# Late modulation vectors of a two-layer diffusion trunk: partial tiles transposed on TensorE, their four groups added by one VectorE instruction

## The chip, the cores and the metric

The kernel runs on one core of a Trainium2 chip. The metric is the device time of one execution in microseconds; the times shown are those of three executions and their median. TensorE (PE), VectorE (DVE), ScalarE (ACT), GpSimd (POOL) and SyncE (SP) each work through a list of instructions of their own and wait for each other by semaphores.

## What is computed

The reference is one step of a trunk of two layers over 384 tokens (128 of a prompt, 256 of a sample) with 1024 channels. Each layer has a token-mixing part with four branches (mLSTM, neighbourhood attention, differential attention, Mamba-2 scan) and an expert part of 16 experts. Both are modulated by six vectors per layer, which come from a conditioning vector, one for the prompt tokens and one for the sample tokens:

```python
def modulation(cvec, w_ada, b_ada):
    m = (jax.nn.silu(cvec) @ w_ada + b_ada)[:, None, :]
    return jnp.split(m, 6, axis=-1)

def trunk_layer(x, cvec, p, lam_init, ctx):
    shift1, scale1, gate1, shift2, scale2, gate2 = modulation(cvec, p['w_ada'], p['b_ada'])
    h = rms_norm(x, p['norm1_w']) * (1 + scale1) + shift1
    ...
    x = x + gate1 * (mixed @ p['w_out'])
    h2 = rms_norm(x, p['norm2_w']) * (1 + scale2) + shift2
    x = x + gate2 * expert_choice_ffn(h2, p['w_router'], p['w_gate'], p['w_up'], p['w_down'])
```

The product with w_ada (1024 by 6144) is what the change is about: columns 2048 to 6143, which give gate1, shift2, scale2 and gate2. All arithmetic is fp32 or split fp32 (a high and a low part).

## The kernel before

The kernel is written by hand for each engine; the order of the work is the order of the lines, and semaphores join the engines.

A layer runs so: modulated norm, input projection (seven tiles of w_in), neighbourhood attention (10 units), differential attention (12 units), two scans (mLSTM, SSD) with their states, the branch norms on VectorE, the transposes of the branches (L1211), the branch and output projections, the router, and 16 experts whose weights stream in by DMA.

Between the units of attention and scans TensorE takes jobs, in the order of JOB_SITES. A letter names the kind: g is one of 32 gate tiles of 128 columns (24 matmuls of the split weights, L781), p ("part") is one of eight w_ada tiles of 512 columns, s ("sum") finishes the tile of the same number. The order is s0 with the first attention unit, s1 and s2 with two later ones, s3 in the first scan, s4 at its state, s5 in the second scan, s6 at the second state, s7 in the tail, where only jobs are left on TensorE while VectorE does the branch norms.

A part (ada_partial, L787) multiplies 32 columns, of which two hold the conditioning vectors and 30 are zero, by the tile. The eight chunks of 128 rows are spread over four groups of 32 columns of the array, two chunks each, so that row 32 g + r of the bank holds group g's share for vector r. ScalarE copies the bank to SBUF (MPL). A sum (ada_sum, L793) then takes each 128 columns of that copy as weights against adasel, a constant of 128 by 2 with ones in the rows 32 g + r: this adds the four groups and turns the result, and leaves 2 columns per 128 channels, 8 in all. ScalarE copies these 8 columns to mod (take_job, L1447). The first four w_ada tiles of a layer go by ada_early and ada_select, with the same ada_sum; of the 24 sums of the program 16 are jobs.

After each gate job ScalarE (L1595) takes the result, stores it, and writes the high part of the next weight quarter (high_parts, L1447); GpSimd then subtracts it from the weights to leave the low part (L722), which TensorE needs four quarters later. ScalarE's job copies stand in its queue between the exponentials of attention and scans.

On VectorE the branch norms end at L2271 (br_ready), for which TensorE's transposes of L1211 wait. Next VectorE waits for the copy of sum 7, adds the bias to mod (L2275), forms the scale (L2277) and halves two vectors (L2278, L2279); then it forms the low parts of the transposed branches (L2286), each after ScalarE's copy of the high part, for which the branch matmuls (L781 on the operand named work_fp32r) wait. mod is next used by L2311, after the output projection. L2239 to L2271 are the last steps of the branch norms; L2260 adds the state's share of the scan to its output. rowp holds the layer's row parameters; its columns lambda and m0 (128 each) are read before the attention units begin, and the next layer's are loaded over them after the router.

Of the kernel before, what the change touches and what calls it, by code (L numbers as in the profile page):

```python
# [22 lines left out]
ALU = mybir.AluOpType  # L23
ACT = mybir.ActivationFunctionType
AX = mybir.AxisListType
# [19 lines left out]
ROW, _at = {}, 0  # L45
# [98 lines left out]
EARLY = 4  # L144
# [125 lines left out]
def trunk_program(nc, dr, outs):  # L270

    (y_prompt, y_sample, new_na_k, new_na_v, new_diff_k, new_diff_v, new_C, new_n, new_m, new_ssm) = outs
    with ExitStack() as ctx:
# [6 lines left out]
        dve_step = ctx.enter_context(nc.semaphore("dve_step"))  # L280
# [7 lines left out]
        PS = ctx.enter_context(nc.psum_tensor("banks", [128, 8, 512], F32))  # L288
# [20 lines left out]
        rowp = sb("rowp", [128, NROW])  # L309
        colp = sb("colp", [128, NCOL])  # L310
        c32 = sb("c32", [128, KC, 32])
        mod = sb("mod", [128, 48, 2])
# [9 lines left out]
        def RP(name):  # L322
            o, w = ROW[name]
            return rowp[:, o:o + w]

        def CP(name):
            o, w = COL[name]
            return colp[:, o:o + w]
# [92 lines left out]
        def MPL(i):  # L421

            return KRAW if i < 3 else NAQK[:, 1:3, 256:512]
# [84 lines left out]
        ident = K("ident")  # L508
# [3 lines left out]
        def over(ap, axis, n):  # L512

            v = ap.unsqueeze(axis)
            shape = list(v.shape)
            shape[axis] = n
            return v.broadcast_to(shape)

        def job_bank(j):

            return 3 if j == 0 else j % 2
# [248 lines left out]
        def _(pe):  # L770
# [20 lines left out]
            def ada_sum(bank, partial):  # L791
                for j in range(4):
                    mm = pe.matmul(PS[:, bank, 2 * j:2 * j + 2], partial[:, j // 2, 128 * (j % 2):128 * (j % 2) + 128], K("adasel"), start=True, stop=True)  # L793
                return mm

            def ada_early(layer, i, keys):


                for j in range(i, i + 2):
                    w = tile(keys[j - i])  # L800
                    if i:
                        pe.wait_ge(sem["ada_taken"], EARLY * layer + j - 1)
                    ada_partial(ada_bank(layer, j), w).then_inc(sem["ada_part"], 1)
# [20 lines left out]
            for g in range(6):  # L824
                t, h = g // 2, g % 2
                for c in range(4):
                    mm = pe.transpose(PS[:, g, c * 128:(c + 1) * 128], XIN[:, t, (4 * h + c) * 128:(4 * h + c + 1) * 128], ident)
# [9 lines left out]
            for l in range(L):  # L837
# [6 lines left out]
                for k in range(KC):  # L844
                    pe.wait_ge(sem["hl_odd" if k % 2 else "hl_ready"], 4 * l + k // 2 + 1)
                    mm = three_passes(PS[0:24, 7, 0:T], (WSMH[:, k, :], wsm[:, k, :]), h_in(k), k == 0, k == KC - 1)
# [52 lines left out]
                for t in range(TT):  # L899
                    mm = pe.transpose(PS[:, 7, 24 * t:24 * t + 24], GRAW[0:24, t * 128:(t + 1) * 128], ident[0:24, 0:24])  # L900
# [9 lines left out]
                for i in range(3):  # L910
                    mm = turn3(4 + i, lambda t: ROWS[:, i, t * 128:(t + 1) * 128])
# [7 lines left out]
                for c in range(4):  # L919
                    mm = pe.transpose(PS[:, 6, c * 128:(c + 1) * 128], KRAW[:, c // 2, (c % 2) * 128:(c % 2) * 128 + 128], ident)  # L920
# [4 lines left out]
                def job():  # L925

                    j = jobs[0]
                    jobs[0] += 1
                    kind, i = JOBS[j]
                    if j >= 2:  # L930
                        pe.wait_ge(sem["job_evac"], NJ * l + j - 1)
                    else:
                        pe.wait_ge(sem["proj_evac"], N_PROJ * l + (19, N_PROJ)[j])
                    if kind == "sum":
                        pe.wait_ge(sem["job_evac"], NJ * l + JOBS.index(("part", i)) + 1)
                        mm = ada_sum(job_bank(j), MPL(i))
                    elif kind == "part":
                        mm = ada_partial(job_bank(j), tile(("mix", l, 7 + [t_[:2] for t_ in JOB_TILES].index(("ada", i)))))
                    else:
                        hi, lo_ = next_quarter()[0]  # L940
                        for k in range(KC):
                            mm = three_passes(PS[:, job_bank(j), 0:T], (hi[:, k, :], lo_[:, k, :]), h_in(k), k == 0, k == KC - 1)
                    mm.then_inc(sem["job_out"], 1)
# [14 lines left out]
                for t, b in ((0, 7), (1, 4), (2, 5)):  # L958
                    for c in range(4):
                        mm = pe.transpose(PS[:, b, c * 128:(c + 1) * 128], NAQK[:, t, c * 128:(c + 1) * 128], ident)  # L960
# [177 lines left out]
                for i, (t, d, b, bq) in enumerate(((0, 0, 2, None), (0, 1, 3, None), (1, 0, 4, 5), (1, 1, 6, 7), (2, 0, 2, 3), (2, 1, 4, 5))):  # L1138
                    if i >= 4:
                        pe.wait_ge(sem["num_evac"], 9 * l + i - 2)  # L1140
                    for h in range(4):
                        mm = over_keys(PS[:, b, 65 * h:65 * h + 65], h, [(d, ks, off) for ks, off in SEEN[d][t]], lambda _, ks: V1[:, ks, h, :])
                    if bq is not None:
                        for ch in range(2):
                            mm = pe.matmul(PS[:, bq, 130 * ch:130 * ch + 130], QKT[:, ch, t * 128:(t + 1) * 128], C0[:, ch, d, :], start=True, stop=True)
# [3 lines left out]
                for c in range(2):  # L1149
                    mm = pe.transpose(PS[:, 6, c * 128:(c + 1) * 128], QKT[:, 2 + c, 0:128], ident)  # L1150
# [5 lines left out]
                for d in range(2):  # L1156
                    for h in range(4):
                        mm = pe.matmul(PS[0:64, 7 if d == 0 else 2, 65 * h:65 * h + 65], KW[:, d, h, :], V1[:, 0, h, :], start=True, stop=True)
# [28 lines left out]
                for g, b in ((0, 4), (1, 7)):  # L1187
                    for t in (1, 2):
                        o = 256 * (t - 1)
                        mm = pe.matmul(PS[:, b, o:o + 256], XS[64 * g:64 * g + 64, 3, t * 128:(t + 1) * 128], H0[64 * g:64 * g + 64, :], start=True, stop=True)  # L1190
# [254 lines left out]
        def _(act):  # L1445
            def copy(dst, src, scale=1.0):
                return act.activation(dst, src, ACT.Copy, scale=scale)  # L1447
# [48 lines left out]
            for l in range(L):  # L1496
# [29 lines left out]
                j = [0]  # L1526
# [55 lines left out]
                def take_job(split=True):  # L1582

                    j = jobs[0]
                    jobs[0] += 1
                    kind, i = JOBS[j]
                    act.wait_ge(sem["job_out"], NJ * l + j + 1)
                    if kind == "part":
                        ins = copy(MPL(i), PS[:, job_bank(j), :].rearrange("p (a b) -> p a b", a=2))
                    elif kind == "sum":  # L1590
                        ins = copy(mod[:, 4 * (EARLY + i):4 * (EARLY + i) + 4, :], PS[:, job_bank(j), 0:8].rearrange("p (a b) -> p a b", a=4))
                    else:
                        if 8 <= i:
                            act.wait_ge(spilled[i % 8], 16 * (SPILLED // 8 * l + i // 8))
                        ins = act.activation(GATES[:, i % 8, :], PS[:, job_bank(j), 0:T], ACT.Tanh, scale=0.5)  # L1595
                    ins.then_inc(sem["job_evac"], 1)
                    if j and JOBS[j - 1][0] == "gate" and JOBS[j - 1][1] < SPILLED:
                        g = JOBS[j - 1][1]
                        act.wait_ge(sem["job_evac"], NJ * l + j)
                        act.dma_start(spill[l, g % 8, :, g // 8, :], GATES[:, g % 8, :]).then_inc(spilled[g % 8], 16)  # L1600
                    if split:
                        high_parts(AHEAD[j])
# [208 lines left out]
        def _(dve):  # L1811
            steps = [0]

            def step():

                steps[0] += 1
                return steps[0]
# [28 lines left out]
            for l in range(L):  # L1846
# [425 lines left out]


                dve.wait_ge(sem["job_evac"], NJ * l + JOBS.index(("sum", 7)) + 1)
                TTo(mod[:, 16:48, :], mod[:, 16:48, :], over(CP("b_ada")[:, 16:48], 2, 2), ALU.add).then_inc(dve_step, 1)  # L2275
                dve.wait_ge(dve_step, step())
                STT(amp[:, 1, :, :], mod[:, 32:40, :], 1.0, over(CP("norm2"), 2, 2), ALU.add, ALU.mult)  # L2277
# [174 lines left out]
```

## Time and profile before

| | us |
|---|---|
| median of 3 executions | 1950.98 (1949.69 to 1955.09) |
| span of the profiled execution, first to last instruction | 1947.9 |
| TensorE busy | 1760.1 (90%) |
| VectorE busy | 639.0 (33%) |
| ScalarE busy | 548.0 (28%) |
| GpSimd busy | 514.4 (26%) |
| mean granted TensorE clock | 0.994 |

The profiled execution's own time outside the profiler isn't given; its span stands 3.1 us below the median. In the rows below times count from the span's start. A timeline row has start, duration, engine, line, operation, output and inputs, shapes, and the number of instructions that it merges; a bracket at its end is the idle time of the engine before it and what ended it. A TensorE matmul of fp32 operands is recorded as two passes, each with a weight load (PEld), a transpose as one.

### The profile page before, as it was taken

What the parts mean: (1) busy time and instruction counts of PE and PEld (TensorE: products, weight loads), DVE (VectorE), ACT (ScalarE), POOL (GpSimd) and SP (SyncE); (2) the same over time, 40 slices, a digit from 0 to 9 for tenths busy, and PEclk for the clock granted to TensorE, in tenths of its full rate; (3) what the DMA queues carried; (4) which work ended last, traced back from release to release, by engine and by line L of the source; (5) the groups of instructions that cost most, each with busy time, mean ns of one, the idle gap of its engine ahead of it and who ended that gap; (6) DMA issues with size and microseconds to landing.
All of it is one profiled execution on the core that took longest, in us unless ns stands there. A gap on an engine that the chain in (4) does not pass through costs nothing.

```text
span 1947.9 us, 22784 instructions
## 1 busy us (share of the span) xinstructions
PE 1760.1 (90%) x9204; PEld 1122.5 (58%) x9204; DVE 639.0 (33%) x1385; ACT 548.0 (28%) x1054; POOL 514.4 (26%) x654
## 2 busy tenths in 40 slices
PE   6899999999998788888889999999999988888887
PEld 3788897899442222222258889879975322222223
DVE  1187345873400000001143853558632000000011
ACT  3444444242321110110144444432442111011011
POOL 0787344275100000000037754424830000000000
PEclk9999999999999999999999999999999999999999
DMA  9525533574999999999973354345655999999996
GB/s 351 133 100 184 205 119 131 182 244 177 386 393 429 426 427 427 428 426 427 421 208 130 104 199 168 117 162 175 241 215 239 425 427 426 428 427 427 427 425 274
DMA packets 123545, 567.78 MB, mean 291 GB/s; under 512 B 21809, under 2 KB 31281, under 8 KB 98353
## 3 DMA queue, kind: packets, MB, share of 16 engines
q1 hardware_dynamic: 112656, 543.91, 70.6%
q10 hardware_dynamic: 9920, 20.84, 3.0%
q8 instruction: 73, 1.20, 0.3%
q0 software_dynamic: 864, 1.58, 0.2%
q14 instruction: 32, 0.25, 0.0%
HBM read 550.57 MB, written 15.73 MB: 291 GB/s over the span
## 4 chain that ended last, share of the span: by engine, by line
PE 53%; DMA 35%; DVE 7%; ACT 2%; SPq 1%; issue 1%; POOL 0%; ACTq 0%; DVEq 0%
PE banks L781 29%; PE banks L1342 11%; DMA work<-in_w_gate 8%; DMA ring<-in_w_down 6%; DMA ring<-in_w_up 6%; DMA work<-in_w_up 6%; DMA ring<-in_w_gate 4%; DMA work<-in_w_down 3%; PE banks L787 1%; PE banks L1091 1%; PE banks L1311 1%; DMA ring<-in_w_ada 1%; PE banks L793 1%; ACT work L1447 1%; PE banks L1107 1%
## 5 line engine op out<-in xcount | busy, mean ns | idle before, releaser
L722 POOL TENSOR_TENSOR ring_fp32r<-ring,ring_fp32r 128x256 fp32r<-128x256 f32 x592 | 462.8, 816 | 822.9 <-ACT ring_fp32r L1447 822.2
L1342 PE MATMUL banks<-ring,work 128*64 128x512 f32 x1776 | 402.7, 597 | 77.6 <-DMA ring<-in_w_gate 33.6
L781 PE MATMUL banks<-xT_fp32r,ring_fp32r 128*128 128x384 f32 x1280 | 347.6, 345 | 1.8 <-POOL ring_fp32r L722 1.8
L1447 ACT ACTIVATE work<-banks 32x512 f32<-32x512 f32 (+6 forms) x400 | 202.7, 528 | 449.3 <-PE banks L1342 251.8
L1342 PEld LDWEIGHTS banks<-ring,work 128*64 128x64 f32 x1776 | 122.4, 136 | 336.3 <-issue 198.7
L1342 PE MATMUL banks<-work 128*64 128x512 f32 x972 | 224.1, 597 | 39.2 <-DMA work<-in_w_gate 14.9
L781 PEld LDWEIGHTS banks<-xT_fp32r,ring_fp32r 128*128 128x128 f32 x1280 | 235.9, 191 | 12.8 <-issue 5.3
L781 PE MATMUL banks<-hT_fp32r,ring_fp32r 128*128 128x384 f32 x640 | 216.4, 338 | 0.0
L2364 DVE SCALAR_TENSOR_TENSOR xT<-banks,mod,xT 128x128 f32<-128x128 f32 (+1 forms) x128 | 46.7, 413 | 444.8 <-PE banks L1378 444.5
L1447 ACT ACTIVATE ring_fp32r<-ring 128x1024 fp32r<-128x1024 f32 (+1 forms) x164 | 154.4, 970 | 76.5 <-PE banks L781 66.9
L1342 PEld LDWEIGHTS banks<-work 128*64 128x64 f32 x972 | 67.1, 137 | 178.1 <-issue 111.3
L1762 ACT ACTIVATE work<-banks 128x512 f32<-128x512 f32 x32 | 19.1, 597 | 480.6 <-PE banks L1342 480.6
L781 PE MATMUL banks<-work_fp32r,ring_fp32r 128*128 128x384 f32 x768 | 139.2, 341 | 0.0
L781 PE MATMUL banks<-ring_fp32r,xT_fp32r 128*128 128x512 f32 (+1 forms) x480 | 136.2, 369 | 1.2 <-DVE small L1892 1.2
L781 PEld LDWEIGHTS banks<-work_fp32r,ring_fp32r 128*128 128x128 f32 x768 | 134.6, 189 | 2.7
L781 PEld LDWEIGHTS banks<-hT_fp32r,ring_fp32r 128*128 128x128 f32 x640 | 122.2, 191 | 1.1
L2386 DVE TENSOR_TENSOR work<-work,banks 128x512 f32<-128x512 f32 x32 | 22.0, 688 | 291.5 <-PE banks L1342 291.5
L781 PEld LDWEIGHTS banks<-ring_fp32r,xT_fp32r 128*128 128x128 f32 x480 | 86.7, 189 | 16.0 <-DVE small L1892 1.4
L1342 PE MATMUL banks<-hT,work 128*64 128x512 f32 x324 | 75.2, 599 | 20.5 <-DMA work<-in_w_gate 8.4
L781 PE MATMUL banks<-ring_fp32r,hT_fp32r 128*128 128x512 f32 (+1 forms) x240 | 88.4, 368 | 0.0
L1595 ACT ACTIVATE work<-banks 128x384 f32<-128x384 f32 x64 | 31.4, 490 | 162.1 <-PE banks L781 162.1
L1342 PEld LDWEIGHTS banks<-hT,work 128*64 128x64 f32 x324 | 21.7, 136 | 68.4 <-issue 33.3
(296 smaller groups left out, 1706.7 us busy)
## 6 DMA issues: line engine op xcount, KB each, us to landing
ring<-in_w_up SPq DMA_DIRECT2D x38, 2048.0 KB, 30.6
ring<-in_w_gate SPq DMA_DIRECT2D x37, 2048.0 KB, 30.5
ring<-in_w_down SPq DMA_DIRECT2D x36, 2048.0 KB, 30.0
ring<-in_w_in SPq DMA_DIRECT2D x28, 2048.0 KB, 8.2
ring<-in_w_ada SPq DMA_DIRECT2D x24, 2048.0 KB, 8.5
work<-in_w_down SPq DMA_DIRECT2D x20, 2048.0 KB, 30.5
work<-in_w_gate SPq DMA_DIRECT2D x18, 2048.0 KB, 30.5
work<-in_w_up SPq DMA_DIRECT2D x16, 2048.0 KB, 30.6
```

What stands on the lines that cost most here:

```text
L722: ins = pool.tensor_tensor(rounded(w_), w_, rounded(hi_), ALU.subtract)
L781: mm = pe.matmul(dst, a_, b_, start=(first and i == 0), stop=(last and i == 2))
L787: mm = pe.matmul(PS[32 * g:32 * g + 32, bank, :], c32[:, k, :], w[:, k, :], start=(k < 4), stop=(k >= 4), tile_position=(0, 32 * g))
L793: mm = pe.matmul(PS[:, bank, 2 * j:2 * j + 2], partial[:, j // 2, 128 * (j % 2):128 * (j % 2) + 128], K("adasel"), start=True, stop=True)
L1091: pe.matmul(PS[:, 4 + c % 4, 0:T], ident[:, r:r + 1].broadcast_to([128, 128]), ROWS[:, 0, :], start=True, stop=True)\
L1107: mm = pe.matmul(dst, PM[:, 2 * h + d, off:off + 128], v(d, ks), start=(i == 0), stop=(i == len(pairs) - 1))
L1311: mm = pe.matmul(dst, rounded(strided(part[:, t, 512 * (q // 8):512 * (q // 8) + 512], q // 2 % 4)), rounded(SEL[:, t, a:b, :].rearrange(" ...
L1342: mm = pe.matmul(dst[64 * hf:64 * hf + 64, :], x(k), w[kk][:, 512 * hf:512 * hf + 512], start=(k == 0), stop=(k == KC - 1), tile_position= ...
L1447: return act.activation(dst, src, ACT.Copy, scale=scale)
L1595: ins = act.activation(GATES[:, i % 8, :], PS[:, job_bank(j), 0:T], ACT.Tanh, scale=0.5)
L2364: ins = STT(xT[:, dc, a:b], PS[:, bank, a:b], mod[:, 40 + dc, g:g + 1], xT[:, dc, a:b], ALU.mult, ALU.add)
L2386: TTo(HH[:, e % 2, :], SA, PS[:, 2 * (e % 2) + 1, :], ALU.mult).then_inc(sem["hh_ready"], 1)
```

## The change

The 16 sums that are jobs become transposes. TensorE turns the four chunks of 128 columns whole (ada_turn), into the full bank. ScalarE copies columns 32 g and 32 g + 1 of each chunk, 32 columns in all, to MODP, which is the place of lambda and m0 in rowp (256 columns for eight tiles). When the eight are there, VectorE adds the four groups of all tiles into mod in one reduction, ahead of the bias. The early sums stay as they are.

```diff
--- before.py
+++ after.py
@@ -322,6 +322,8 @@
         def RP(name):
             o, w = ROW[name]
             return rowp[:, o:o + w]
+
+        MODP = rowp[:, ROW["lambda"][0]:ROW["lambda"][0] + 256]
 
         def CP(name):
             o, w = COL[name]
@@ -793,6 +795,11 @@
                     mm = pe.matmul(PS[:, bank, 2 * j:2 * j + 2], partial[:, j // 2, 128 * (j % 2):128 * (j % 2) + 128], K("adasel"), start=True, stop=True)
                 return mm
 
+            def ada_turn(bank, partial):
+                for j in range(4):
+                    mm = pe.transpose(PS[:, bank, 128 * j:128 * j + 128], partial[:, j // 2, 128 * (j % 2):128 * (j % 2) + 128], ident)
+                return mm
+
             def ada_early(layer, i, keys):
 
 
@@ -933,7 +940,7 @@
                         pe.wait_ge(sem["proj_evac"], N_PROJ * l + (19, N_PROJ)[j])
                     if kind == "sum":
                         pe.wait_ge(sem["job_evac"], NJ * l + JOBS.index(("part", i)) + 1)
-                        mm = ada_sum(job_bank(j), MPL(i))
+                        mm = ada_turn(job_bank(j), MPL(i))
                     elif kind == "part":
                         mm = ada_partial(job_bank(j), tile(("mix", l, 7 + [t_[:2] for t_ in JOB_TILES].index(("ada", i)))))
                     else:
@@ -1588,7 +1595,8 @@
                     if kind == "part":
                         ins = copy(MPL(i), PS[:, job_bank(j), :].rearrange("p (a b) -> p a b", a=2))
                     elif kind == "sum":
-                        ins = copy(mod[:, 4 * (EARLY + i):4 * (EARLY + i) + 4, :], PS[:, job_bank(j), 0:8].rearrange("p (a b) -> p a b", a=4))
+                        turned = PS[:, job_bank(j), :].rearrange("p (a b) -> p a b", a=16)[:, :, 0:2]
+                        ins = copy(MODP[:, 32 * i:32 * i + 32].rearrange("p (a b) -> p a b", a=16), turned)
                     else:
                         if 8 <= i:
                             act.wait_ge(spilled[i % 8], 16 * (SPILLED // 8 * l + i // 8))
@@ -2272,6 +2280,8 @@
 
 
                 dve.wait_ge(sem["job_evac"], NJ * l + JOBS.index(("sum", 7)) + 1)
+                dve.tensor_reduce(mod[:, 16:48, :], MODP.rearrange("p (a g b) -> p a b g", g=4, b=2), AX.X, ALU.add).then_inc(dve_step, 1)
+                dve.wait_ge(dve_step, step())
                 TTo(mod[:, 16:48, :], mod[:, 16:48, :], over(CP("b_ada")[:, 16:48], 2, 2), ALU.add).then_inc(dve_step, 1)
                 dve.wait_ge(dve_step, step())
                 STT(amp[:, 1, :, :], mod[:, 32:40, :], 1.0, over(CP("norm2"), 2, 2), ALU.add, ALU.mult)
```

## Rows read from the trace of the kernel before

**Rows 1.** The page, part 4: the chain that ended last, by engine.

```profile
PE 53%; DMA 35%; DVE 7%; ACT 2%; SPq 1%; issue 1%; POOL 0%; ACTq 0%; DVEq 0%
```

**Rows 2.** Stretches of layer 0 from attention to the jobs' end.

```profile
core 0: us, PE busy (x) PEld busy (x) DVE busy (x) ACT busy (x) POOL busy (x), PEclk, DMA share, GB/s
180.00:235.00 55.00, 55.00 (x355) 47.77 (x354) 21.77 (x56) 25.52 (x59) 22.28 (x30) 0.97 0.53 185
...
360.00:385.00 25.00, 25.00 (x186) 20.27 (x185) 22.53 (x62) 6.67 (x12) 7.23 (x9) 1.00 0.46 168
385.00:408.00 23.00, 22.77 (x138) 22.36 (x135) 21.71 (x45) 5.40 (x10) 13.72 (x17) 1.00 0.68 195
```

**Rows 3.** All matmuls of L793: ns, minimum/median/maximum.

```profile
L793 PE MATMUL banks<-cst,work x192: 167/251/318, 25.8 to 1343.5; 128*128 128x2 f32 x192
```

**Rows 4.** Timeline of TensorE, attention, layer 0 (us: start, duration).

```profile
217.50 0.44 PE L781 MATMUL banks<-xT_fp32r,ring_fp32r 128*128 128x384 f32 x1
...
221.77 0.49 PE L991 MATMUL banks<-cst,work 128*128 128x128 f32 x3
...
223.66 1.05 PE L793 MATMUL banks<-cst,work 128*128 128x2 f32 x8
224.57 0.52 PE L991 MATMUL banks<-cst,work 128*128 128x128 f32 x3
...
226.49 0.45 PE L781 MATMUL banks<-xT_fp32r,ring_fp32r 128*128 128x384 f32 x1
```

**Rows 5.** Timeline of TensorE in the second scan, layer 0.

```profile
358.97 0.95 PE L793 MATMUL banks<-cst,work 128*128 128x2 f32 x8
359.78 1.54 PE L1091 MATMUL banks<-work,cst 128*128 128x384 f32 x4
```

**Rows 6.** Timeline of all engines at the end of the jobs, layer 0.

```profile
407.13 0.49 ACT L1595 ACTIVATE work<-banks 128x384 f32<-128x384 f32 x1 [3.67 <-PE banks L781]
...
407.33 2.84 PE L1211 MATMUL banks<-cst,work 128*128 128x128 f32 x24 [0.23 <-DVE work L2271]
...
409.60 3.02 ACT L1447 ACTIVATE work_fp32r<-banks 128x512 fp32r<-128x512 f32 x6
...
410.29 3.68 DVE L2286 TENSOR_TENSOR work_fp32r<-banks,work_fp32r 128x512 fp32r<-128x512 f32 x6 [2.51 <-ACT work_fp32r L1447]
...
414.20 6.14 PE L781 MATMUL banks<-work_fp32r,ring_fp32r 128*128 128x384 f32 x34
```

**Rows 7.** Timeline of VectorE in the second scan, layer 0, with its idle time.

```profile
362.70 0.15 DVE L2151 COPY small<-work 128x1 f32<-128x1 f32 x1 [0.92 <-PE banks L1083]
```

**Rows 8.** Timeline of VectorE and GpSimd in the tail, layer 0.

```profile
391.25 3.62 DVE L2260 TENSOR_TENSOR work<-work 128x256 f32<-128x256 f32 x2
391.29 2.83 POOL L722 TENSOR_TENSOR ring_fp32r<-ring,ring_fp32r 128x256 fp32r<-128x256 f32 x4
...
396.17 1.61 POOL L722 TENSOR_TENSOR ring_fp32r<-ring,ring_fp32r 128x256 fp32r<-128x256 f32 x2 [2.04 <-ACT ring_fp32r L1447]
...
396.61 0.57 DVE L2260 TENSOR_TENSOR work<-work 128x256 f32<-128x256 f32 x1
```

**Rows 9.** ScalarE copies by shape: count, busy time, mean ns.

```profile
L1447 ACT ACTIVATE work<-banks 128x384 f32<-128x384 f32 x46 | 22.0, 489 | 32.1 <-PE banks L781 31.9
...
L1447 ACT ACTIVATE mod<-banks 128x8 f32<-128x8 f32 x24 | 4.1, 169 | 22.3 <-PE banks L793 21.9
```

**Rows 10.** One VectorE reduction: duration in ns, minimum/median/maximum.

```profile
L2050 DVE TENSOR_REDUCE small<-work x4: 420/420/421, 188.9 to 1142.3; 128x2 f32<-128x256 f32 x4
```

**Rows 11.** TensorE's clock (PEclk, columns as in rows 2), both layers.

```profile
227.00:228.00 1.00, 1.00 (x5) 1.00 (x4) 0.77 (x2) 0.10 (x1) 0.00 (x0) 0.50 0.00 0
...
1162.00:1163.00 1.00, 1.00 (x4) 1.00 (x4) 0.00 (x0) 0.10 (x2) 0.94 (x2) 0.50 0.03 8
```

**Rows 12.** Timeline of TensorE, layer 1: what opens and follows a gate job.

```profile
1159.98 0.69 PE L781 MATMUL banks<-xT_fp32r,ring_fp32r 128*128 128x384 f32 x1
...
1166.79 0.49 PE L991 MATMUL banks<-cst,work 128*128 128x128 f32 x3
```

## The prediction

> **What bounds the kernel now.** I began with the chain that ended last [rows 1]: TensorE has 53% of it and DMA 35%, the latter in the expert stages, where weights stream in. The change lies before them, in the gate and modulation jobs of each layer, so the question there is whether TensorE is the bound. The stretches answer it [rows 2]: from 180 to 235 us TensorE is busy for 55.00 of 55.00 us, from 360 to 385 for 25.00 of 25.00, and only from 385 to 408 it idles, for 0.23 us of 23. In that last stretch VectorE is busy for 21.71 us, and what TensorE waits for at its end is VectorE (L2271, the last product of the branch norms) [rows 6]. So two engines take turns: TensorE sets the time up to the second scan, VectorE after it. The point of exchange is 362.70 [rows 7], the last time that VectorE waits for TensorE, 0.92 us. From there to 407.3 it works without a wait for another engine. Layer 1 has the same order of events.
>
> What comes after the norms moves as a block: TensorE needs the transposed branches, then gate job 31, then the branch matmuls, and the weight streams of the experts start on semaphores that these set. A microsecond gained before is a microsecond of the end.
>
> **The sums on TensorE (removed) against transposes (added).** A sum is four fp32 matmuls of two columns, each recorded as two passes (192 records for the 24 sums of the program) [rows 3]. Starts tell its price: 223.66 to 224.57 is 0.91 us in attention [rows 4], 358.97 to 359.78 is 0.81 in the second scan [rows 5]. A 128 by 128 fp32 transpose has one record: 24 of them take 2.84 us [rows 6], 0.118 each, so four take 0.47. A sum that turns gives back 0.44 or 0.34 us; I take 0.42, since most sums stand like the first.
>
> Sixteen of the 24 sums change, eight per layer. Sums 0 to 5 lie before VectorE's last wait, so they are on the path: 6 x 0.42 = 2.5 us per layer, 5.0 in both. Is there a VectorE bound hidden between? Its smallest margin is the 0.92 us at 362.70; sum 5, right ahead of it, takes at most 0.44 of it, and the others move both engines together. So nothing is late next before 362.70. Bounds for the term: 12 x 0.34 = 4.1 and 12 x 0.44 = 5.3.
>
> Sums 6 and 7 lie after it, in the stretch that VectorE ends. They free 0.8 us per layer of TensorE, which is worth nothing unless VectorE ends earlier too.
>
> **VectorE's tail, which the change moves without touching it.** At 391.25 VectorE starts two adds of 256 columns (L2260); 0.04 us later GpSimd starts four subtractions of the weight split [rows 8]. The pair of adds takes 3.62 us. The next pair begins 0.44 us into a GpSimd piece (396.61 after 396.17), and its first add takes 0.57. So the meeting at 391.25 costs about 3.62 - 2 x 0.57 = 2.5 us, on the path, and it hangs on 0.04 us of order. GpSimd's start goes back to TensorE (job, ScalarE's high part, GpSimd), and TensorE runs 0.4 us earlier against VectorE once sum 6 is shorter. GpSimd would then be in the middle of a piece when the add arrives, as at 396.61, and the add waits for a piece, not for four. I take the stall as gone, since the one other row of this meeting shows it so, and charge up to 1 us for new meetings, as GpSimd's other pieces move too. VectorE's end then comes 1.5 us earlier, more than the 0.8 that TensorE has freed plus its present wait of 0.23; TensorE collects its 0.8 per layer, 1.6 in both. Bounds: 0 (stall stays) to 2.1 (2 x 0.8 and both waits of 0.23). A new stall of the same kind is a rival.
>
> On this the Trainium skill (SBUF: State Buffer, "Who interferes with whom") says that VectorE and GpSimd take turns at one shared pair of ports, each holding it for a whole instruction. By that rule alone the add would wait for one piece (2.83 / 4 = 0.71 us), and the pair would take under 2 us; the trace has 3.62, so here the rule is too mild, and the row decides.
>
> **What is added.** VectorE gets one reduction of 256 elements to 64 per layer and a step of its semaphore. The nearest row, 256 elements to 2, is 0.42 us [rows 10]; I take it, and 0.2 to 0.8 (half and double) as bounds for the other stride and the 64 results. It waits for sum 7's copy and stands before the bias addition, the three small steps and the six low parts of the branches (L2286), for which TensorE's branch matmuls wait. The cover is VectorE's idle 2.51 us before L2286, in which ScalarE is still at weight splits and starts its branch copies only at 409.60 [rows 6]. So it costs nothing; without cover 2 x 0.46 = 0.9 us. ScalarE's copies grow from 8 to 32 columns: (489 - 169) / 376 = 0.85 ns per column [rows 9], 24 x 0.85 = 20 ns each, 0.16 us per layer, on an engine that waited 3.67 us before its last job copy [rows 6]. Nothing. The order of DMAs and the bytes stay.
>
> **The clock.** TensorE's granted clock is at 1.2 GHz (0.50) at 227 us and at 1162 us [rows 11], both times behind a passage with two attention units and a sum but no gate job; in layer 0 it lasts from 221.77 to 226.49 [rows 4]. A gate job under the low clock takes 1159.98 to 1166.79, 6.81 us [rows 12], against 217.50 to 221.77, 4.27 [rows 4]: 2.5 us lost in layer 1 and, the fall there being shorter, about half that in layer 0: 3.8 together. There are four such passages (sums 1 and 2 of each layer), and each gets 0.44 us shorter. I count 0 for the forecast: which passages fall is a matter of phase.
> The Trainium skill (TensorE: Matmul & The Clock Gate, "Part 4: PE-mode transpose") speaks against the change: transposes do not count as TensorE being busy for the clock. The 24 transposes in a row [rows 6] are no fall, so the trace doesn't bear it out for a few transposes; I keep it as a rival.
>
> **Sum.** 5.0 + 1.6 = 6.6 us. The profiled execution has a span of 1947.9 us, 3.1 below the median of 1950.98, which holds start and end outside the span. 1947.9 - 6.6 = 1941.3 for the span, 1950.98 - 6.6 = 1944.4 for the time. That is 0.34%; about 0.3%, 5.9 us, is what a measurement of this kernel can tell from no change.
>
> **Rivals.**
> - A, the stall stays or is replaced by one as long: sums 6 and 7 give nothing, 5.0 us, 1946.0. For it: the cause of the stall isn't known beyond one meeting per layer. Chance 0.25.
> - B, fewer clock falls, since the passages shorten: the forecast less 3.8, 1940.6. For it: both falls followed these passages. Chance 0.12.
> - C, more falls (the page's rule), in all four passages: two more at up to 2.5 us, 1944.4 + 3.8 to 5.0, about 1949. Chance 0.10.
> - D, slower: GpSimd's pieces, now early, starve VectorE at two or more places of the tail. The price is 2.5 us a meeting, all of it on the path, since VectorE ends the tail already. The 5.0 us are used up once VectorE's tail grows by 2.5 us per layer; from there on the change is slower. Three meetings in place of one add 5.0 per layer: 10.0 - 5.0 = +5.0, 1956.0. Against it: one long meeting per layer among many overlaps. Chance 0.04.
> - E, transposes are no cheaper in place (they pay two passes, or a change of mode around them): 0, 1951. Against it: the 24 in rows 6. Chance 0.04.
> The forecast has 0.45. Faster by over 0.3%: two thirds of the forecast's 0.45 (it is only 0.7 us beyond the bound), a third of A, all of B: 0.50. Slower by over 0.3%: part of D, 0.04. The rest, 0.46, is within. The range takes in A, B and C: 1939.5 to 1949.5.
>
> **What the profile after would show.** Sums of four records and about 0.47 us; the waits of VectorE for TensorE up to the second scan still there, the last near 0.5 us or more; L2260 at 0.6 us or less each; TensorE's wait before L1211 gone (forecast) or about 1.1 us (A); VectorE still idle before L2286. The prediction is wrong if TensorE's wait before L1211 exceeds 1.5 us, if the low-clock time in the passages doubles, or if VectorE's waits before 362.70 vanish.

## The result, and the profile after

| | before | after |
|---|---|---|
| median of nine executions, us | 1950.98 (1948.08 to 1957.75) | 1941.62 (1939.39 to 1946.59) |
| ratio, 95% interval | | 0.9948 (0.9937 to 0.9960) |
| span of the profiled execution, us | 1947.9 | 1944.8 |
| mean granted clock of the profiled execution | 0.994 | 0.989 |

The change makes the kernel 0.52% faster, 10.1 us by the ratio (7.8 to 12.3) and 9.4 us by the medians. The forecast was 1944.4 us; the time lies in the range, 2.8 us below the forecast. The two profiles must not be subtracted: the profiled execution after is the slowest of its nine (1946.59 us), and the one before is, by its clock of 0.994 against a mean of 0.9909, a fast one of its kernel. The low clock also falls at different places in the two: after, it lasts 17.1 us at a stretch near 30 us, where the profile before had two stretches of 3.4 us. So I compare stretches, not ends.

The page's chain of the kernel after, by engine (part 4). VectorE's share was 7% and TensorE's 53% [rows 1]:

```profile
PE 58%; DMA 36%; DVE 3%; ACT 2%; SPq 1%; issue 0%; POOL 0%; ACTq 0%; DVEq 0%
```

The matmuls of the new helper (line L800 in the kernel after; from L325 on the lines stand 2 to 10 further on) answer to [rows 3]: 64 records for 16 turns, four each instead of eight.

```profile
L800 PE MATMUL banks<-cst,work x64: 270/273/329, 190.0 to 1338.8; 128*128 128x128 f32 x64
```

The timeline of TensorE after, in attention of layer 0: from the turn to the next group of transposes 224.56 to 225.06 is 0.50 us, where [rows 4] had 0.91.

```profile
224.56 0.66 PE L800 MATMUL banks<-cst,work 128*128 128x128 f32 x4
225.06 0.49 PE L998 MATMUL banks<-cst,work 128*128 128x128 f32 x3
```

VectorE and GpSimd after, in the tail of layer 0 (timeline). VectorE's last wait for TensorE in the second scan is 0.47 us (0.92 in [rows 7]). GpSimd's four pieces now begin 0.50 us ahead of the pair of adds (L2268, formerly L2260), not 0.04 behind it [rows 8], and the pair takes 1.40 us, not 3.62.

```profile
360.44 0.15 DVE L2159 COPY small<-work 128x1 f32<-128x1 f32 x1 [0.47 <-PE banks L1090]
...
388.89 1.40 DVE L2268 TENSOR_TENSOR work<-work 128x256 f32<-128x256 f32 x2
...
402.22 0.96 DVE L2279 TENSOR_TENSOR work<-work,rowp 128x768 f32<-128x768 f32 x1
403.09 0.41 DVE L2283 TENSOR_REDUCE mod<-rowp 128x64 f32<-128x256 f32 x1
...
407.53 3.68 DVE L2296 TENSOR_TENSOR work_fp32r<-banks,work_fp32r 128x512 fp32r<-128x512 f32 x6 [3.39 <-ACT work_fp32r L1454]
```

```profile
388.39 3.38 POOL L724 TENSOR_TENSOR ring_fp32r<-ring,ring_fp32r 128x256 fp32r<-128x256 f32 x4
```

The branch norms end at 402.22 + 0.96 = 403.18, and TensorE begins its transposes (L1218) at 404.17 with no wait; it had waited 0.23 us for them [rows 6]. From the last wait in the scan to the end of the norms VectorE takes 42.7 us; it was 44.6 (362.70 to 407.3, [rows 6, 7]). VectorE is now 1.0 us early and TensorE alone sets the time there. TensorE after:

```profile
404.17 2.78 PE L1218 MATMUL banks<-cst,work 128*128 128x128 f32 x24
...
411.31 8.86 PE L783 MATMUL banks<-work_fp32r,ring_fp32r 128*128 128x384 f32 x49 [0.18 <-issue]
```

Here is a wait that was not there. From the transposes to the first branch matmul it was 414.20 - 407.33 = 6.87 us [rows 6] and is 411.31 - 404.17 = 7.14. The low parts of L2296 above end at 411.21, right ahead of the matmul.

**Where the time went, stage by stage.** A stage's gain is the distance between two landmarks of TensorE's timeline (first instruction of the next stage) before, less the same after. Positive is faster.

| us gained by TensorE | layer 0 | layer 1 | what it holds |
|---|---|---|---|
| sum 0, ahead of attention | 0.39 | 0.38 | one turn |
| attention | 2.46 | 4.03 | two turns, and the clock |
| differential attention and first scan | 0.38 | -1.31 | one turn, and in layer 1 the clock |
| second scan and tail, to the branch transposes | 1.70 | 1.59 | four turns |
| from there to the first sum of squares behind the branch matmuls (L813 before) | -0.35 | -0.35 | the new wait |

Attention is where the low clock was: the stretches of [rows 11] are at 1.00 after, and the whole of attention too. The same two stretches of both layers, before and then after (columns as in [rows 2]):

```profile
205.00:235.00 30.00, 30.00 (x194) 27.23 (x194) 9.55 (x30) 13.05 (x30) 8.99 (x13) 0.94 0.38 128
1140.00:1195.00 55.00, 55.00 (x343) 48.88 (x341) 16.51 (x52) 23.17 (x59) 20.51 (x31) 0.94 0.56 202
```

```profile
205.00:235.00 30.00, 30.00 (x204) 26.97 (x203) 10.82 (x35) 14.63 (x34) 10.08 (x15) 1.00 0.47 162
1140.00:1195.00 55.00, 55.00 (x356) 48.75 (x355) 17.87 (x58) 24.18 (x63) 20.54 (x31) 1.00 0.57 206
```

TensorE is busy for all of both. At 0.94 they hold 194 and 343 matmul records, at 1.00 204 and 356, although a turn has four records where a sum had eight.

### The profile page after: what moved, and what is told of

Same layout as the page of the kernel before. It is cut to its first block, busy times and chain, and to the rows that moved or that the text cites. A ratio compares the mean times of both kernels' runs of the same rounds, so it can differ in the third digit from the quotient of the medians.

```text
span 1944.8 us, 22658 instructions
## 1 busy us (share of the span) xinstructions
PE 1760.6 (91%) x9140; PEld 1119.2 (58%) x9140; DVE 636.9 (33%) x1387; ACT 548.6 (28%) x1054; POOL 517.1 (27%) x654
## 4 chain that ended last, share of the span: by engine, by line
PE 58%; DMA 36%; DVE 3%; ACT 2%; SPq 1%; issue 0%; POOL 0%; ACTq 0%; DVEq 0%
PE banks L783 32%; PE banks L1349 11%; DMA work<-in_w_gate 8%; DMA ring<-in_w_up 6%; DMA work<-in_w_up 6%; DMA ring<-in_w_down 6%; DMA ring<-in_w_gate 4%; DMA work<-in_w_down 3%; PE banks L789 2%; PE banks L1114 1%; PE banks L1098 1%; PE banks L1318 1%; DMA ring<-in_w_ada 1%; ACT work L1454 1%; PE banks L1075 1%; PE banks L1054 1%
```

## The experiments

All times are medians, all ratios to the kernel before on the same chip, with 95% intervals. Since the low clock comes and goes from execution to execution, I also give a difference "at equal clock": a least-squares fit over all 192 executions of this study, each with its time and mean granted clock, with a level for each kernel and one common slope. The slope is -1.10 us for each 0.001 of clock, with 1.5 us of scatter. The kernel before has a mean clock of 0.9909 in 74 executions; the change has 0.9929 and is 7.9 +- 1.05 us faster at equal clock.

### Half of the change: the sums on TensorE's path (e1), and the two in VectorE's tail (e2)

Each job chooses its helper by its tile; the reduction covers the tiles that are turned.

```diff
-                        mm = ada_turn(job_bank(j), MPL(i))
+                        mm = (ada_turn if i in (0, 1, 2, 3, 4, 5) else ada_sum)(job_bank(j), MPL(i))
```

> Sums 0 to 5 of each layer are transposed, 6 and 7 stay matmuls by adasel. Theory P (path by TensorE, as predicted): 12 x 0.42 us = 5.0 us less, ratio 0.9974, and VectorE's long add of the tail (3.1 us) stays, since GpSimd and VectorE keep their distance; TensorE still waits some 0.2 us for the branch norms. Rival F (the shorter passages in attention also save low-clock time): up to 3.8 us more, 8.8 us less, ratio 0.9955.

Measured: 1943.99 against 1952.58, 0.9963 (0.9951 to 0.9976), at equal clock -5.75 +- 0.95 us, mean clock 0.9924. The stall stays, and so does TensorE's wait of 0.23 us. VectorE, then GpSimd, then TensorE in this kernel's timeline, layer 0:

```profile
389.23 3.62 DVE L2270 TENSOR_TENSOR work<-work 128x256 f32<-128x256 f32 x2
```

```profile
389.26 2.84 POOL L724 TENSOR_TENSOR ring_fp32r<-ring,ring_fp32r 128x256 fp32r<-128x256 f32 x4
```

```profile
405.30 2.84 PE L1218 MATMUL banks<-cst,work 128*128 128x128 f32 x24 [0.23 <-DVE work L2281]
```

By the stages of its trace the six turns give 0.39, 0.92, 0.38 and 0.81 us in a layer. The 0.92 is the kernel after (attention takes 39.66 us) against experiment f4 below (40.58 us), which has sums there and, in its profile, no low clock in attention. That is 2.50 per layer and 5.0 in both, as in the prediction's sum.

> Only sums 6 and 7 are transposed. Theory P with the stall gone: GpSimd starts 0.45 us earlier against VectorE, the long add falls to about 1 us, VectorE ends its norms before TensorE, and TensorE collects 0.9 us per layer less some 0.3 us that it then waits for the low parts of the branches: 1.2 us in both layers, ratio 0.9994. Rival A (the stall stays, or TensorE's time there is not on the path): 0, ratio 1.0000. If rival F is right, this one shows none of the gain beyond, as it leaves the attention passages alone.

The edit is the same with (6, 7). Measured: 1949.38, 0.9983 (0.9974 to 0.9991), at equal clock -1.7 +- 0.9. The stall goes with these two turns alone. VectorE's timeline in layer 0, and GpSimd's:

```profile
391.04 1.42 DVE L2270 TENSOR_TENSOR work<-work 128x256 f32<-128x256 f32 x2
```

```profile
390.55 3.38 POOL L724 TENSOR_TENSOR ring_fp32r<-ring,ring_fp32r 128x256 fp32r<-128x256 f32 x4 [0.16 <-ACT ring_fp32r L1454]
```

So it is sum 6 that places GpSimd against VectorE, as the prediction said, and the early sums shift both alike. Up to the branch transposes this kernel gains 0.90 us in each layer. Then it gives some back: in layer 0 the branch matmuls start with a wait of 1.08 us, since ScalarE, now early, waits for the branch weights to land before it can split them. TensorE's timeline, then ScalarE's:

```profile
414.37 3.93 PE L783 MATMUL banks<-work_fp32r,ring_fp32r 128*128 128x384 f32 x21 [1.08 <-issue]
```

```profile
407.81 0.63 ACT L1454 ACTIVATE ring_fp32r<-ring 128x512 fp32r<-128x512 f32 x1 [0.79 <-DMA ring<-in_w_branch]
```

The two halves add up: -7.2 and -3.3 us by the ratios make 10.5, against 10.1 for the whole.

### The sums done twice (e3, e4)

```diff
-                        mm = ada_sum(job_bank(j), MPL(i))
+                        for _ in range(2 if i in (6, 7) else 1):
+                            mm = ada_sum(job_bank(j), MPL(i))
```

> The kernel before with sums 6 and 7 of each layer issued twice (the second rewrites the same result). It adds 0.85 us per sum to TensorE in the tail, 1.7 us per layer. Theory P: 0.2 us of it are covered by the wait for VectorE, 2 x 1.5 = 3.0 us more, ratio 1.0015. If the tail were VectorE's alone with room to spare: 0. The long add may vanish here too, as GpSimd moves by 0.9 us the other way; that alone saves nothing, because TensorE then is the last.

Measured: 1965.69, 1.0068 (1.0050 to 1.0086), 13.3 us slower.

> The kernel before with sums 3, 4 and 5 issued twice, none of them in an attention passage. Theory P: all on TensorE's path, 6 x 0.87 us = 5.2 us more, ratio 1.0027. If a sum costs more than its slot on TensorE (a delay of those that wait for it), more than 5.2; if part of the stretch up to the second scan is VectorE's or ScalarE's, less.

Measured, with (3, 4, 5): 1962.11, 1.0054 (1.0041 to 1.0067), 10.5 us slower. Both misses are of one kind. Four and six more sums at 0.91 us are 3.6 and 5.5 us, and the rest is clock: the mean clock falls to 0.9838 and 0.9868, worth (0.9909 - 0.9838) x 1.10 / 0.001 = 7.8 us and 4.5 us. That makes 11.4 of 13.3 us and 10.0 of 10.5. Right behind the doubled sum 6 (its last two-column matmul starts at 373.78) TensorE is at 1.2 GHz from 376 to 390 us in layer 0. The stretches of the first kernel:

```profile
376.00:377.00 1.00, 1.00 (x7) 1.00 (x7) 0.97 (x2) 0.00 (x0) 1.00 (x2) 0.57 0.06 25
377.00:389.00 12.00, 12.00 (x62) 11.07 (x62) 10.94 (x32) 0.00 (x0) 1.82 (x2) 0.50 0.01 2
389.00:390.00 1.00, 1.00 (x9) 0.88 (x8) 0.96 (x3) 0.30 (x1) 0.00 (x0) 0.60 0.00 0
390.00:391.00 1.00, 1.00 (x7) 1.00 (x6) 0.97 (x3) 0.29 (x1) 0.00 (x0) 1.00 0.00 0
```

This turned the question: not "what do the turns save" alone, but "what do they do to the clock".

### A slot as long as before, filled with transposes (f1)

```diff
-                        mm = ada_turn(job_bank(j), MPL(i))
+                        for _ in range(2):
+                            mm = ada_turn(job_bank(j), MPL(i))
```

> The changed kernel with each of the 16 late turns issued twice (eight transposes, about 0.94 us, the slot that a sum had). TensorE's work is then about that of the kernel before, so every theory agrees on the work: 0 to 1 us more than before. They differ on the clock. Theory L (the low clock follows how long TensorE goes without gate matmuls, whatever stands there): mean clock as before, 0.991, ratio 1.000. Theory T (transposes count less for the clock than the two-column matmuls): a lower mean clock than before and a ratio above 1.002. Theory K (transposes count more): mean clock 0.993 as in the changed kernel, ratio 0.998.

Measured: 1949.64 against 1952.56, 0.9985 (0.9976 to 0.9993), so 2.9 us faster (1.4 to 4.7) with nothing taken off TensorE. That the slots are as long as before is in the stages: sum 0's differs by 0.06 us, and the second scan and tail by 0.01 and 0.02 us. Attention alone is shorter, by 1.59 us in layer 0 and 3.15 in layer 1, and there the low clock is gone (columns as in [rows 2]):

```profile
205.00:235.00 30.00, 30.00 (x208) 27.06 (x206) 10.20 (x34) 14.39 (x32) 10.63 (x16) 1.00 0.43 150
1140.00:1195.00 55.00, 55.00 (x360) 48.81 (x360) 17.88 (x58) 24.57 (x63) 21.22 (x32) 1.00 0.58 211
```

The mean clock over its eleven executions is 0.9925. Part of the regained time is lost again at another place: this profile has the low clock at the end of differential attention, at 305 and 1257 us, where the kernel before had none, and that stage is 1.67 and 1.66 us longer. These falls are of another kind than those in attention: from 300 to 305 us, ahead of the first, TensorE idles for 1.33 us. It does so in the kernel after too, and there the clock stays at 1.00, so the idle time alone doesn't decide. The stall is back too, as the slot's length decides it: GpSimd starts 0.03 us behind the add, and the pair takes 3.60 us.

```profile
391.37 3.60 DVE L2269 TENSOR_TENSOR work<-work 128x256 f32<-128x256 f32 x2
```

```profile
391.40 2.82 POOL L724 TENSOR_TENSOR ring_fp32r<-ring,ring_fp32r 128x256 fp32r<-128x256 f32 x4
```

### Turns in attention alone (f2), and in the scans alone (f3)

> Only sums 1 and 2, those between two attention units without a gate job, are transposed. The work: 4 x 0.44 = 1.8 us less, ratio 0.9991, at an equal clock. If the clock's part of the gain sits in these passages: 2 to 3 us beyond it, ratio 0.9978, and a mean clock of 0.993 against 0.991. If it sits elsewhere: nothing beyond.

> Only sums 3 to 5, in the first scan, at its state and in the second scan, are transposed. The work: 6 x 0.42 = 2.5 us less, ratio 0.9987, at an equal clock. If the low clock of the kernel before sits in the scans too (the kernel with sums 3 to 5 twice showed 13.7 us of it at the second state of layer 1): up to 3 us beyond it, and a higher mean clock; else nothing beyond.

The edit is that of the first experiment with (1, 2) and with (3, 4, 5). Measured: 1948.76, 0.9986 (0.9977 to 0.9995), and 1949.91, 0.9985 (0.9975 to 0.9995); at equal clock both are 2.6 +- 0.9 us faster, at mean clocks of 0.9915 and 0.9908. The work is 4 x 0.44 = 1.8 and 2 x (0.38 + 0.81) = 2.4 us. The times don't separate the two. They don't settle either what the expectation asked of f2: the interval holds both 0.9991 (the work alone) and 0.9978 (with the clock), and the mean clock of 0.993 that the clock's part called for didn't come. The traces do separate them: with turns in attention there is no low clock there, with turns in the scans it is there three times, as with sums.

### The two-column matmuls of attention done twice (h1)

> The kernel before with sums 1 and 2, in the attention passages without a gate job, issued twice. The work: 4 x 0.9 us = 3.6 us more, ratio 1.0018 at an equal clock. Theory M (two-column matmuls in these passages let the clock fall): more low-clock time than before, mean clock 0.989 or less against 0.991, low clock behind three or four of the four passages of the profiled execution, and 2 us or more beyond the work. Rival: the falls are chance, the mean clock stays 0.991 and only the 3.6 us are seen.

The edit is that of the doubled sums with (1, 2). Measured: 1963.30 against 1951.81, 1.0057 (1.0043 to 1.0071), 11.1 us slower, mean clock 0.986. The added work is 4 x 0.91 = 3.6 us. The low clock now follows each of the four passages. Stretches of this kernel, both layers:

```profile
208.00:212.00 4.00, 4.00 (x16) 3.85 (x15) 1.30 (x4) 1.17 (x3) 2.79 (x4) 0.57 0.05 14
229.00:236.00 7.00, 7.00 (x23) 6.59 (x22) 1.62 (x5) 0.71 (x2) 0.07 (x1) 0.51 0.06 24
1164.00:1172.00 8.00, 8.00 (x33) 7.47 (x33) 1.62 (x5) 2.95 (x7) 2.79 (x4) 0.57 0.20 72
1188.00:1195.00 7.00, 7.00 (x24) 6.47 (x24) 1.62 (x5) 1.10 (x3) 0.52 (x1) 0.51 0.09 30
```

TensorE is busy for the whole of each before and in them: the clock fell although the engine never idled. Counted over 14 profiled executions (the change is there twice, as after and h2), at the four passages of each:

| jobs 1 and 2 are | profiles | passages followed by the low clock |
|---|---|---|
| sums (two-column matmuls) | before, e2, e3, e4, f3, f4, h1 | 2, 2, 2, 3, 3, 0, 4: 16 of 28 |
| turns (transposes) | after, e1, f1, f2, g1, g2, h2 | 0 of 28 |

The passages of one profile are not independent: before, e2, e3, e4, f3 and f4 run the same program up to the end of attention in layer 0, and there show 1, 0, 1, 1, 1 and 0 falls. So with sums a fall is a matter of chance from execution to execution; by profiles it is six of seven against none of seven. The mean clock, which every execution has, says the same more weakly: 0.9922 over the 66 executions with turns in attention, 0.9910 over the 109 with single sums there (before, e2, f3, f4). The difference of 0.0011 +- 0.0006 is worth 1.2 +- 0.6 us by the slope of the fit.

### The low part of the weights first (f4)

> The kernel before, with one more quarter's low part on GpSimd ahead of the DMAs of the mLSTM state, so that its four subtractions begin as soon as ScalarE's high part is there, some 0.2 us earlier. Theory: they are then in progress when VectorE's add (L2261) arrives, the add takes under 1 us instead of 3.1, and VectorE ends the branch norms some 2 us earlier; but TensorE ends its jobs only 0.2 us before VectorE does in the kernel before, so the time falls by 0 to 0.5 us, ratio 1.000. If the stall itself were worth its 2.5 us per layer: 5 us less, ratio 0.9974.

The kernel before with one call moved ahead, so that GpSimd's pieces start earlier in the tail:

```diff
+                low_parts(AHEAD[41])
```

Measured: 1952.27, 1.0004 (0.9993 to 1.0015). The stall is gone (the pair starts 0.20 us into a GpSimd piece and takes 1.71 us), and TensorE reaches the branch transposes 0.40 us earlier in each layer, without a wait. Then the branch matmuls start 0.46 us late in layer 0 (0.90 in layer 1). VectorE, then TensorE, layer 0:

```profile
390.93 1.71 DVE L2261 TENSOR_TENSOR work<-work 128x256 f32<-128x256 f32 x2
```

```profile
406.58 2.78 PE L1212 MATMUL banks<-cst,work 128*128 128x128 f32 x24
...
414.00 4.28 PE L782 MATMUL banks<-work_fp32r,ring_fp32r 128*128 128x384 f32 x23 [0.46 <-issue]
```

From the branch transposes to the first sum of squares it is 0.63 us longer in layer 0 and 1.04 in layer 1, which uses up the gain. Taken away by itself, the stall of 2.5 us is worth nothing here.

### What is next behind (g1, g2, and the change again, h2)

> The changed kernel with VectorE's reduction issued three times. 2 x 0.46 us more per layer on VectorE, ahead of the low parts of the branches. VectorE idles 3.4 us there and ends the norms 1.0 us before TensorE: 0, the same time as the changed kernel (ratio to before 0.9948). If the reduction were on the path: 1.8 us more, 0.9957.

```diff
+                for _ in range(2):
+                    dve.tensor_reduce(mod[:, 16:48, :], MODP.rearrange("p (a g b) -> p a b g", g=4, b=2), AX.X, ALU.add).then_inc(dve_step, 1)
+                    dve.wait_ge(dve_step, step())
```

> The changed kernel, with the branch matmuls started after five of the six high and low parts; the sixth, which only the second half of the first channel block needs, is waited for there. It takes away TensorE's new wait of 0.2 us per layer ahead of them: 0.4 to 0.6 us less than the changed kernel, ratio to before 0.9945, within the noise of the times; the profile shows it as no idle time before the first branch matmul. If the wait was for the low part of the weights instead, it stays.

The second lets the branch matmuls begin when five of the six low parts are there, and waits for the sixth where it is first read:

```diff
-                pe.wait_ge(sem["brt_lo"], 6 * (l + 1))
+                pe.wait_ge(sem["brt_lo"], 6 * l + 5)
+                        if dc == 0 and nb == 2:
+                            pe.wait_ge(sem["brt_lo"], 6 * (l + 1))
```

(and the same for brt_evac). The change itself ran once more beside the last of these experiments:

> The changed kernel once more, beside the other three of this call. Ratio to before 0.9948 as measured, mean clock 0.993. Theory M: no low clock between 190 and 240 us or between 1140 and 1195 us. If the falls there are chance at the rate of the kernels with sums (12 behind 24 passages of six profiled executions), two of the four passages show one.

Measured: 1943.66 with two more reductions, 0.9959 (0.9946 to 0.9973); 1944.12 with the late sixth part, 0.9958 (0.9943 to 0.9972); 1943.45 for the change again, 0.9954 (0.9941 to 0.9968), at equal clock -7.0 +- 1.0, -7.8 +- 1.0 and -5.95 +- 1.4. Three kernels, one time. The reduction is covered. The sixth part is seen only in the trace: the branch matmuls follow without a wait,

```profile
405.53 2.78 PE L1218 MATMUL banks<-cst,work 128*128 128x128 f32 x24
...
412.32 5.96 PE L783 MATMUL banks<-work_fp32r,ring_fp32r 128*128 128x384 f32 x33
```

6.79 us behind the transposes' start, and the last line of the table of stages becomes +0.07 and +0.10: 0.42 and 0.45 us regained, 0.9 in both layers, below what these intervals can tell. I have no version that is shown to beat the change.

## Why the prediction was right, and where it was short

The time lies in the stated range, but that range was 10 us wide. The forecast's own 6.6 us lies below the interval of the gain, 7.8 to 12.3 us: the sum was short, by a term that it had put at nothing.

1. **The sums on the path.** Right in kind and size: 5.0 us foretold, 5.0 by the stages, 5.75 +- 0.95 at equal clock. The waits of VectorE for TensorE stayed, the last at 0.47 us, as foretold (0.5 or more; the prediction put it a little high). One reading was wrong without harm: 0.92 us is not VectorE's smallest margin. It waits only 0.47 and 0.45 us for TensorE at 338.31 and 345.51 us, but the turns ahead of these move both engines, and the waits are 0.46 and 0.45 after. Rival E is out: four transposes take 0.50 us in their place.
2. **Sums 6 and 7, and the stall.** Right in mechanism: the pair of adds takes 1.4 us (0.52 and 0.84, where 0.6 or less each was foretold), TensorE's wait ahead of the branch transposes is gone, and the kernels with a short slot for sum 6 (after, e2) or an earlier start of GpSimd (f4) lose the stall, and so does e3, whose longer slots and low clock put GpSimd 2.8 us behind the add; with slots as long as before it stays (e1, f1, f2, f3, h1, and e4 in layer 0). Rival A is out, and D, since no second long meeting came; the small ones are in VectorE's cover of 1.0 us. The size was a little high. "TensorE collects its 0.8 per layer": it did, 0.89 and 0.79 (the fourth line of the table less e1's 0.81 and 0.80), and then gave back 0.35 in each layer to the new wait. The prediction had named VectorE's idle time before L2286 as the cover of the reduction, 2.51 us, and not asked what that idle time hangs on. It hangs on ScalarE, whose chain begins at the end of a gate job of TensorE; with TensorE's own wait of 0.23 us gone, this chain of copy, four splits and six high parts, with VectorE's low parts behind it, ends last. So 1.0 us, not 1.6.
3. **The reduction.** Right: 0.41 us for a term of 0.42, hidden, and two more of them don't show. Copies of 32 columns mean 185 ns against 169 [rows 9], 16 for an estimate of 20.
4. **The clock, counted as 0.** This is the step that failed. The prediction wrote "which passages fall is a matter of phase" and gave the case of fewer falls (rival B, 3.8 us) a chance of 0.12. The runs show that it is no matter of phase alone: 16 of 28 passages with sums, none of 28 with turns. The experiment with slots as long as before measures the term most nearly by itself: 2.9 us (1.4 to 4.7). Its profile fits: 1.59 + 3.15 = 4.7 us regained in attention, less what comes back at the end of differential attention, 1.7 us a time, seven times in the eight profiles without low clock in attention. The size is less sure than the sign: the mean clocks of all executions give only 1.2 +- 0.6 us.

The sum with these sizes: 5.0 + 1.0 + 2.9 = 8.9 us, against 10.1 (7.8 to 12.3). The forecast had 5.0 + 1.6 + 0 = 6.6. The forecast and rival B came true together.

The prediction also took the 3.1 us between span and median for start and end outside the span. In the executions of the record the span is 1.7 to 2.8 us (median 1.8) below the time of the same execution; so the profiled one, whose own time isn't given, was faster than the median. The forecast of the time doesn't use it, the one of the span does.

**Rival C**, that transposes leave the clock worse off, is refuted for this kernel. The first thing to see is the two experiments of equal and of doubled length: eight transposes in the slot, no low clock in any passage; eight two-column matmuls (sixteen passes) in it, low clock behind all four. Only behind that stands the rule of the Trainium skill (TensorE: Matmul & The Clock Gate, "Part 4: PE-mode transpose") that a transpose "doesn't count as PE-busy the same way" for the clock. This case's traces don't bear it out for four or eight fp32 transposes among other matmuls: 0 of 28 passages with 1.2 GHz, a mean clock of 0.9925 with the transposes done twice against 0.9909. What in the two-column matmuls lets the clock fall isn't settled by these runs; only that in attention it is they, and not idle time of the engine, which is nil there.

**What stays open.** At equal clock the change is 7.9 +- 1.05 us faster, and its second series 5.95 +- 1.4, where the stages give 6.0. The one number is too high for the stages, the other isn't; and the experiment with equal slots is 1.1 +- 0.95 us faster at equal clock, where the stages give nothing. The mean clock weighs every period alike, while a period of 3.4 us costs 1.6 us where TensorE sets the time and may cost nothing where the weights stream. So the fit may leave part of the clock's gain in the kernels' levels. That is argued, not shown.

## What to carry to other kernels

An fp32 sum over groups of partitions with only two columns to stream was dear on TensorE twice over in this kernel: in time (eight passes of 0.11 us for four matmuls), and, by chance from execution to execution, in the clock of what follows. Turn the operand with a transpose and add on an engine that idles; then measure the slot's length and the clock separately, for which a kernel with the slot filled up to its old length is the cheapest instrument. And before counting a cover, ask what the idle time hangs on: it may shrink with the very microseconds that are saved.

## What the runs showed of the hardware

- A VectorE add of 256 columns that takes 0.42 us alone took 3.1 to 3.2 us when it started 0.03 to 0.05 us ahead of four GpSimd pieces in a row [rows 8], and so in e1, e4, f1, f2, f3 and h1 again; the same pair that began 0.5 us into a piece took 1.4 us in all, and 0.2 us into it 1.71 us. It is not being first as such that costs: in e3 an add that started 0.22 us ahead of GpSimd (395.47 against 395.69) took its 0.42 us. Why the near tie is so dear stays open.
- TensorE went to 1.2 GHz while it was busy without a gap, for 3.4 us up to 13.7 us at a stretch, behind two-column fp32 matmuls (in attention, and behind doubled sums in e3 and e4). It also went there at the end of differential attention, behind 1.33 us of idle time in five, in some profiles and not in others.
- Executions of one kernel differ in mean granted clock by up to 0.008, and 0.001 of it is 1.1 us of 1950. A span of one profile doesn't tell kernels apart that differ by 0.5%; the stages do.
